# Mixture-of-experts stage of a decoder step: bias rows in four partition groups, the gate read from its bank, gated products moved up, gathers that leave empty slots out

## The reference

```python
logits = (t @ router_w) + router_b
top_v, top_e = lax.top_k(logits, TOP_K)              # 4 of 32 experts for each token
gate = jax.nn.softmax(top_v, axis=-1)
def run_block(tok, g, e):                            # the tokens of one expert
    gu = t_pad[tok] @ w_up[e] + b_up[e]              # (tokens, 2048)
    a = jnp.minimum(gu[:, :D_FF], SWIGLU_LIMIT)      # gate part, limit 7
    u = jnp.clip(gu[:, D_FF:], -SWIGLU_LIMIT, SWIGLU_LIMIT)
    y = ((u + 1.0) * a * jax.nn.sigmoid(1.702 * a)) @ w_down[e] + b_down[e]
    return y * g[:, None]
out = h + sum over the experts of each token of its y
```

## Time and profile before

| | before |
|---|---|
| median of three runs | 1878.54 us |
| the profiled execution's own time | 1879.48 us |
| its span (first to last instruction) | 1877.7 us |
| TensorE matmul (PE) busy | 1830.7 us, 97% |
| TensorE weight load (PEld) busy | 1502.2 us, 80% |
| VectorE (DVE) busy | 1502.5 us, 80% |
| ScalarE (ACT) busy | 1129.8 us, 60% |
| GpSimd (POOL) busy | 245.0 us, 13% |

### The profile page before, as it was taken

The page is one execution under the profiler, slowest core; times in us unless marked ns, Lnnn a source line. Parts: engine busy times, 40 slices in busy tenths (PEclk is TensorE's granted clock), DMA queues, the critical chain, the costliest instruction groups (busy, mean ns, idle before and its releaser), DMA issues.

```text
span 1877.7 us, 27455 instructions
## 1 busy us (share of the span) xinstructions
PE 1830.7 (97%) x9813; PEld 1502.2 (80%) x9813; DVE 1502.5 (80%) x1754; ACT 1129.8 (60%) x1126; POOL 245.0 (13%) x259
## 2 busy tenths in 40 slices
PE   7999999999999999999999999999999999999998
PEld 5898988787768677888888888888888888888886
DVE  6865876644367458999999999999999999999995
ACT  5335544442432346767776776776776777677674
POOL 0040000012330133100110010010011001001000
PEclk9999999999999999999999999999999999999999
DMA  5074221123355249999999999999999999999993
GB/s 227 8 245 168 68 76 51 46 84 96 113 151 196 91 154 370 374 379 383 373 377 388 376 369 390 381 366 385 387 370 373 394 368 371 388 386 369 388 368 106
DMA packets 76747, 514.23 MB, mean 274 GB/s; under 512 B 10744, under 2 KB 31296, under 8 KB 50800
## 3 DMA queue, kind: packets, MB, share of 16 engines
q1 hardware_dynamic: 58944, 454.19, 61.5%
q0 software_dynamic: 17584, 58.51, 11.6%
q10 hardware_dynamic: 144, 0.55, 0.1%
HBM read 490.36 MB, written 28.24 MB: 276 GB/s over the span
## 4 chain that ended last, share of the span: by engine, by line
PE 75%; issue 8%; DVE 7%; ACT 6%; DMA 3%; ACTq 0%; DVEq 0%; POOL 0%; SPq 0%; POOLq 0%
PE bank L1153 26%; PE bank L1171 14%; PE bank L703 6%; PE bank L755 5%; PE bank L630 3%; ACT qT_rounded L1558 3%; PE bank L603 3%; PE bank L1002 3%; PE bank L1135 2%; PE bank L1129 1%; DMA ring<-in_w_exp 1%; PE bank L977 1%; DVE slab L2303 1%; DVE slab L2306 1%; PE bank L1145 1%
## 5 line engine op out<-in xcount | busy, mean ns | idle before, releaser
L2256 DVE TENSOR_TENSOR ring_rounded<-ring,wide_rounded 128x2048 fp32r<-128x2048 f32 x192 | 431.4, 2288 | 50.7 <-ACT wide_rounded L1558 50.3
L1153 PE MATMUL bank<-ring_rounded,slab_rounded 128*128 128x512 f32 x1024 | 400.7, 391 | 0.0
L1558 ACT ACTIVATE wide_rounded<-ring 128x2048 fp32r<-128x2048 f32 x192 | 359.8, 1908 | 10.4 <-PE bank L1153 8.8
L1153 PE MATMUL bank<-xn_rounded,slab_rounded 128*128 128x512 f32 x1024 | 327.5, 391 | 0.0
L2256 DVE TENSOR_TENSOR ring_rounded<-ring,xn_rounded 128x2048 fp32r<-128x2048 f32 x128 | 292.9, 2288 | 16.6 <-ACT xn_rounded L1558 16.6
L1171 PE MATMUL bank<-wide_rounded,slab_rounded 128*128 128x512 f32 x768 | 258.9, 398 | 0.0
L1153 PE MATMUL bank<-wide_rounded,slab_rounded 128*128 128x512 f32 x768 | 247.2, 389 | 0.0
L1558 ACT ACTIVATE xn_rounded<-ring 128x2048 fp32r<-128x2048 f32 x128 | 244.0, 1906 | 0.0
L1153 PEld LDWEIGHTS bank<-ring_rounded,slab_rounded 128*128 128x128 f32 x1024 | 192.6, 188 | 41.5
L1153 PEld LDWEIGHTS bank<-xn_rounded,slab_rounded 128*128 128x128 f32 x1024 | 193.1, 189 | 40.4 <-issue 0.8
L2483 POOL DMA_INDIRECT out_y<-slab,small x32 | 85.1, 2659 | 1001.8 <-ACT slab L1633 1001.8
(11 more groups left out here) (463 smaller groups left out, 2989.3 us busy)
## 6 DMA issues: line engine op xcount, KB each, us to landing
ring<-in_w_exp SPq DMA_DIRECT2D x192, 2048.0 KB, 10.8
ring<-in_w_blk SPq DMA_DIRECT2D x40, 512.0 KB, 3.6
slab<-in_w_tok SPq DMA_DIRECT2D x4, 1304.0 KB, 15.4
ring<-in_w SPq DMA_DIRECT2D x8, 512.0 KB, 3.7
ring<-in_w_out SPq DMA_DIRECT2D x2, 2048.0 KB, 13.4
xn<-in_xT SPq DMA_DIRECT2D x4, 520.0 KB, 8.1
ring<-in_k_cmp SPq DMA_DIRECT2D x32, 64.0 KB, 3.5
ring<-in_k_cmp POOLq DMA_DIRECT2D x32, 64.0 KB, 2.7
```

Source lines behind the costliest of these rows:

```text
L1153: r = mm(bank[:, c, :], a[:, 4 * h + k, :], w[:, k, :], start=False, stop=h == 1 and k == 3 and x == 2)
L1558: fn(WH[(2 * c + h) % 6], ring[:, half_of(c, h)], ACT.Copy).then_inc(S["wh_ready"], 1)
L2256: v.tensor_tensor(ring_r[:, half_of(c, h)], ring[:, half_of(c, h)], WHf[(2 * c + h) % 6], ALU.subtract)\
```

## The change

- PE: the four bias matmuls of an expert are issued together ahead of its first chunk. Each uses 32 partitions only: partition group c (32c to 32c+31) of `pick_r` and `bias_r` holds the rows of bank c, 16 experts with a high and a low row each, and `bias_r` has two column halves (`group`) for the experts 0 to 15 and 16 to 31. PE's loop over the experts is split in two for this. The bank waits (`up_read`) stand at the head of an expert, for all four banks, together with one on `sig_ready`.
- ScalarE: `gated` reads the gate from its PSUM bank, before clipping; the clip is applied to the result by VectorE with GATE_LIMIT. It waits for PE (`half_used`) and not for VectorE, and writes one of two SG buffers. `high_half(5, 0)` moves ahead of `turned_hidden` 0.
- VectorE: both `gate_part` are gone. `hidden_part` 1 moves ahead of `low_half(5, 1)`; `low_half(0, 0)` of the next expert moves behind `low_hidden` 1, and `low_rows` ahead of `low_half(0, 1)`. Three DMA waits move out of the loop.
- Ahead of the experts: the bias comes in one DMA of 128 partitions by 1024 and not in two of 32 by 2048. VectorE builds the new selection matrices from the identity (six small operations), then waits for this DMA and adds a constant row selection to it, all before its first `residual`. ScalarE makes one copy of 128x1024, VectorE one operation of 128x1024; the copies of L1579, L1580, L2277 and L2161 go.
- GpSimd: the gathers get a bound, so that a slot number beyond the last token is left out.

```diff
-            def up_chunk(n, c, last_biases=False):
-                pe.wait_ge(S["up_read"], 4 * n + c + 1)
+            def up_bias(c, group):
+                rows = slice(32 * c, 32 * c + 32)
+                mm(bank[:, c, :], pick_r[rows, :], bias_r[rows, group, :], start=True, stop=False)
+
+            def up_chunk(n, c, group, last_biases=False):
+                first = isinstance(n, int) and n == 0
                 if c == 0:
+                    if not first:
+                        pe.wait_ge(S["sig_ready"], 2 * n)
+                        pe.wait_ge(S["up_read"], 2 * n)
                     pe.wait_ge(S["pick_set"], n + 1)
...
-                q = order[c]
-                mm(bank[:, c, :], pick_r, bias_r[:, q * 512:(q + 1) * 512], start=True, stop=False)
+                if first:
+                    if c >= 2:
+                        pe.wait_ge(*((S["ovf_ready"], 1), (S["y0_ready"], 2 * RT - 2))[c - 2])
+                    up_bias(c, group)
+                elif c == 0:
+                    for b in range(4):
+                        up_bias(b, group)
...
             for t in range(RT):        # ScalarE, first tile's turn
...
                 if t == 0:
-                    act.wait_ge(S["bup_in"], 32)
-                    fn(bias_r[0:NE, :], bias_raw[0:NE, :], ACT.Copy).then_inc(S["bias_ready"], 1)
-                    fn(WH[0][NE:2 * NE, :], bias_raw[NE:2 * NE, :], ACT.Copy).then_inc(S["bias_hi"], 1)
+                    act.wait_ge(S["bias_step"], 1)
+                    fn(WH[0][:, 0:D], bias_raw, ACT.Copy).then_inc(S["bias_step"], 1)
...
             def gated(n, hf):
-                act.wait_ge(S["up_read"], 4 * n + 2 * hf + 5)
-                fn(SG, AA, ACT.Gelu_apprx_sigmoid).then_inc(S["sig_ready"], 1)
+                act.wait_ge(S["half_used"], 12 * n + 4 * hf + 14)
+                fn(SG[hf], bank[:, 2 * hf, :], ACT.Gelu_apprx_sigmoid).then_inc(S["sig_ready"], 1)
...
+                high_half(n, 5, 0)
                 turned_hidden(n, 0)
-                high_half(n, 5, 0)
                 gated(n, 1)
...
+            dve.wait_ge(S["bup_in"], 16)
+            v.tensor_scalar(bias_raw, bias_raw, own_chunk[:, 1:2], None, ALU.add).then_inc(S["bias_step"], 1)
             for t in range(RT):
                 residual(t, 0)
...
             def hidden_part(n, hf):
                 dve.wait_ge(S["half_used"], 12 * n + 4 * hf + 16)
-                v.tensor_scalar(UU[hf], bank[:, 2 * hf + 1, :], LIMIT, -LIMIT, ALU.min, ALU.max).then_inc(S["up_read"], 1)
...
+                v.tensor_scalar(UU[hf], bank[:, 2 * hf + 1, :], 1.0 + LIMIT, 1.0 - LIMIT, ALU.min, ALU.max).then_inc(S["up_read"], 1)
...
-                v.scalar_tensor_tensor(UU[hf], UU[hf], 1.0, SG, ALU.add, ALU.mult).then_inc(S["h_ready"], 1)
+                v.scalar_tensor_tensor(UU[hf], SG[hf], GATE_LIMIT, UU[hf], ALU.min, ALU.mult).then_inc(S["h_ready"], 1)
...
-                gate_part(n, 1)
                 dve.wait_ge(y0_out[0], 32)
                 low_hidden(n, 0)
                 low_half(n, 5, 0)
+                hidden_part(n, 1)
                 low_half(n, 5, 1)
-                hidden_part(n, 1)
                 if following:
                     pick_expert(e + 1)
-                    low_half(n + 1, 0, 0)
...
                 low_hidden(n, 1)
                 if following:
+                    low_half(n + 1, 0, 0)
+                    low_rows(n + 1)
                     low_half(n + 1, 0, 1)
-                    low_rows(n + 1)
...
-            for x in (0, 1):
-                dma(bias_raw[x * NE:(x + 1) * NE, :], d["b_up"]).then_inc(S["bup_in"], 16)
+            dma(bias_raw, d["b_up"]).then_inc(S["bup_in"], 16)
...
                 pool.indirect_dma_start(out=GX[par][:, :], out_offset=None, in_=trow[:, :],
-                                        in_offset=bass.IndirectOffsetOnAxis(ap=index, axis=0))\
+                                        in_offset=bass.IndirectOffsetOnAxis(ap=index, axis=0),
+                                        bounds_check=NT - 1, oob_is_err=False)\
```

More of the change, by code:

```diff
@@ L60 @@
 ALPHA = 1.702
+GATE_LIMIT = LIMIT / (1.0 + math.exp(-ALPHA * LIMIT))
 SLOT = 4096
@@ L306, in build @@
         YR = [slab[:, (6 + b) * D:(7 + b) * D] for b in (0, 1)]
-        AA = slab[:, 8192:8704]
-        SG = slab[:, 8704:9216]
+        SG = [slab[:, 8192 + b * 512:8704 + b * 512] for b in (0, 1)]
         UU = [slab[:, 9216 + b * 512:9728 + b * 512] for b in (0, 1)]
         pick_r = slab_r[:, 10304:10432]
-        pick = causal[:, 0:NE]
+        pick = causal[:, 0:NE].rearrange("p (x j) -> p x j", x=2)
+        low_row = causal[:, 3 * NE:3 * NE + 1]
+        own_chunk = causal[:, 3 * NE + 1:3 * NE + 5]
         entall = causal[:, NE:3 * NE].rearrange("p (e x) -> p e x", x=2)
@@ L377, in halves @@
             return bank[:, 2 * pair:2 * pair + 2, 0:n]
-        order = (0, 2, 1, 3)
         def input_pair(m):
@@ L1173, in down_half, with block_of @@
                 r.then_inc(S["half_used"], 1)
-            def block_of(n, par, following, last_biases=False):
+            def block_of(n, par, following, group, last_biases=False):
                 for c in range(3):
-                    up_chunk(n, c, last_biases and c == 0)
+                    up_chunk(n, c, group, last_biases and c == 0)
                 turn_hidden(n, 0)
-                up_chunk(n, 3)
+                up_chunk(n, 3, group)
                 pe.wait_ge(S["y0_ready"], 2 * RT)
@@ L1192, in block_of @@
                 down_half(n, 5, 1)
[L1194 to L1201, removed]
+            pe.wait_ge(S["bias_ready"], 1)
+            block_of(0, 0, True, 0, True)
+            block_of(1, 1, True, 0)
+            with pe.Fori(1, NE // 4) as pair:
+                block_of(2 * pair, 0, True, 0)
+                block_of(2 * pair + 1, 1, True, 0)
+            with pe.Fori(NE // 4, NE // 2 - 1) as pair:
+                block_of(2 * pair, 0, True, 1)
+                block_of(2 * pair + 1, 1, True, 1)
+            block_of(NE - 2, 0, True, 1)
+            block_of(NE - 1, 1, False, 1)
             pe.wait_ge(S["ovf_ready"], 1)
@@ L1204, in _ @@
             with pe.If(most > P):
[L1205 to L1208, removed]
+                for group in range(2):
+                    with pe.Fori(group * NE // 2, (group + 1) * NE // 2) as e:
+                        for b in range(4):
+                            turn_rows(4 * e + (NE + b), b % 2)
+                            block_of(4 * e + (NE + b), b % 2, False, group)
         @block.scalar
@@ L1641, in _ @@
             act.wait_ge(S["bd_done"], 2 * RT)
+            act.wait_ge(t_out[0], 48)
+            act.wait_ge(y0_out[2], 16)
             block_of(0, 0, True)
@@ L2257, in low_half @@
                     .then_inc(S["wl_ready"], 1)
-            one(v.tensor_tensor(pick, ident[:, 0:NE], ident[:, NE:2 * NE], ALU.add))
+            by_side = ident.rearrange("p (g x j) -> p x j g", g=4, x=2)
+            one(v.tensor_reduce(pick, by_side, AX, ALU.add))
+            one(v.tensor_reduce(low_row, pick[:, 1, :], AX, ALU.add))
+            one(v.tensor_tensor(pick[:, 1, :], pick[:, 1, :], pick[:, 0, :], ALU.subtract))
+            one(v.tensor_copy(pick[:, 0, :], pick[:, 1, :]))
+            one(v.tensor_reduce(own_chunk, ident.rearrange("p (g x) -> p g x", g=4), AX, ALU.add))
+            one(v.tensor_tensor(own_chunk[:, 1:2], own_chunk[:, 1:2], own_chunk[:, 3:4], ALU.add))
             one(v.memset(first_oh[1], 0.0))
+            dve.wait_ge(S["bup_in"], 16)
+            v.tensor_scalar(bias_raw, bias_raw, own_chunk[:, 1:2], None, ALU.add).then_inc(S["bias_step"], 1)
             for t in range(RT):
@@ L2365, in _ @@
             first_rows(RT - 1, 1)
+            dve.wait_ge(t_out[0], 48)
+            dve.wait_ge(t_out[1], 32)
+            dve.wait_ge(y0_out[2], 16)
             with dve.Fori(0, NE // 2 - 1) as pair:
```

30 lines of the change are left out of this document (10 added, 20 removed).

## The result

The changed kernel takes 1854.2 us (median of four runs, 1851.96 to 1858.85). The kernel before, beside it on the same chip, takes 1878.36 (1876.52 to 1879.04). The ratio is 0.9871, with a 95% interval of 0.9859 to 0.9883: 24.2 us faster. The forecast was 1860.9, its range 1852 to 1871. Rival D, which differs from the forecast only in that the row groups overlap wholly, gave 1854.5. That it lies 0.3 from the measured time is partly luck: other terms were off by more than that, and cancelled.

A forecast was written before the change was run, and what follows sets the result against it. The prediction took PE to bound the kernel, with DMA close behind. Its terms, 11.5 + 1.2 + 3.2 + 1.7 = 17.6 us off 1878.54, gave 1860.9 us, range 1852 to 1871.

The forecast's parts named there:

- Rival D: Bias matmuls: the four row groups overlap wholly, gaining 9.6 us and not 3.2, kernel 1854.5 us; chance 0.20.
- The wait (11.5): PE's second turn in each expert: the reorder removes its 0.37 us wait for VectorE's product, 11.5 us gained.
- What is late next is PE itself: Second turn: once VectorE's product comes earlier, nothing but PE holds the path; 0.37 x 31 gained.
- The bias matmuls (3.2): Head of each expert: four 32-partition matmuls cost 0.82 us where four full ones cost 0.92; 3.2 us gained in all.
- The working's 0.94: Bias matmuls: the group's cost in us if each matmul also waited for its own weight load of 0.1.
- The 0.69 of the prediction's side sentence: Bias matmuls: group cost in us by the skill's factor plus the 0.39 drain, a 7 us win.
- The first expert (1.2): First expert's second turn: the reorder and two clips less remove a stall of 1.17 us, 1.2 gained.
- The router (1.7): Ahead of the experts: 2.7 us gained by fewer bias copies, 1.0 lost by waiting for the bias DMA, net 1.7.
- the 1.0 to be lost behind the waiting VectorE: First tile: ScalarE's second sum of squares starts at 624.5, not 623.6, behind VectorE's DMA wait; 1.0 us lost.
- the 2.7 of the copies: First tile's turn: ScalarE's two bias copies, 1.80 + 1.91 us, become one of 1.0; 2.7 gained.
- The gathers (0): GpSimd's gathers: leaving out empty slots relieves DMA by 0 to 1.1 us an expert, worth nothing on PE's path.
- rival B: Experts: DMA takes over as the bound, with a floor of 35.9 us an expert, kernel 1870 us; chance 0.15.

The follow-up runs named there:

- e5: Changed kernel with VectorE's `hidden_part` 1 back behind `low_half(5, 1)`: 1853.84 us, ratio 0.9864.
- e6: Changed kernel with ScalarE's `high_half(5, 0)` back behind `turned_hidden` 0: 1853.09 us, ratio 0.9860.
- e7: Changed kernel with both moves undone, `hidden_part` 1 behind `low_half(5, 1)` and `high_half(5, 0)` behind `turned_hidden` 0: 1867.94 us, ratio 0.9939.
- e10: Kernel before with only ScalarE's `high_half(5, 0)` moved ahead of `turned_hidden` 0: 1868.28 us, ratio 0.9945.
- e9: Kernel before with only VectorE's `hidden_part` 1 moved ahead of `low_half(5, 1)`: 1904.34 us, ratio 1.0136.
- e1: Changed kernel with all four bias matmuls in partition group 0: 1874.22 us, ratio 0.9977.
- e3: Changed kernel with each 32-partition bias matmul at the head of its own chunk: 1915.87 us, ratio 1.0201.
- e12: Changed kernel with the first expert's four bias matmuls issued in two pairs, not one at each chunk: 1850.71 us, ratio 0.985.
- e8: Changed kernel with the next expert's four bias matmuls issued right behind `turn_rows`, not at the head of their own expert: 1854.44 us, ratio 0.9866.
- e4: Changed kernel with the gathers unbounded again, all 128 rows fetched, empty slots too: 1855.74 us, ratio 0.988.

## Why the prediction was right, and where it was not

**The wait (11.5): size exact, account incomplete.** 0.37 an expert went, as said. The working put it to `hidden_part` 1 ahead of `low_half(5, 1)` and called `high_half(5, 0)` only the helper. The runs show two independent ways: in the changed kernel each of them suffices (e5, e6, e7), and on the kernel before `high_half(5, 0)` alone does it (e10), while `hidden_part` 1 alone loses 25 us (e9). The weak step is "What is late next is PE itself". It is so in the changed kernel, but the working looked only at who reads `low_half(5, 1)`; it did not ask what else moves back behind the product. In e9 that is `low_hidden` 1, and PE waits for it. The working neither priced nor named as cover that `low_half(0, 0)` moves behind it.

**The bias matmuls (3.2): mis-sized, 31 x 0.28 = 8.7 measured.** The price of the form was read rightly from the earlier trace rows: 0.39 there, 0.42 here. Taken too high was what the four add: 0.43 was chosen between 0.23 and 0.92, and they add 0.22 to 0.23, the end for whole overlap. (The working's 0.94, for a wait for each weight load, is not the sum of its parts: 0.39 + 0.23 and three or four times 0.1 are 0.92 or 1.02. Nothing hangs on it.) That is rival D, which got a chance of 0.20 for want of a row. It explains most of the distance between 1860.9 and 1854.2: 30 x (0.28 - 0.10) = 5.4. The Trainium skill ("TensorEngine Tiling (Array Packing)", Key Properties) says that a change of tiling mode drains the engine. The price of some 0.42 for each change of form in e1 and e3 agrees with that; that it is a drain no run shows. The factor 3.07 of the Trainium skill ("TensorE: Matmul & The Clock Gate", Measured speedup vs the span model) would give 0.30 for the group, and 0.64 was measured. The 0.69 of the prediction's side sentence, which adds the 0.39, is closer; rival D's 0.62 is closest.

**The first expert (1.2): failed.** The wait of the earlier trace rows did go, but the turn came no earlier. From the first bias matmul to the second turn, before and after, by the busy time of the engines:

```profile
713.58:745.41 31.83, 30.86 (x124) 23.42 (x123) 29.62 (x24) 21.57 (x15) 10.85 (x7) 0.95 0.91 367
```

```profile
706.24:738.35 32.11, 32.11 (x124) 23.42 (x124) 27.35 (x20) 21.50 (x15) 8.32 (x7) 0.95 0.88 335
```

At the same granted clock it is 31.83 with the wait and 32.11 without it. PE's own way there grew from 30.71 (the last matmul's start and 0.23) to 32.11, because here the four bias matmuls stand apart, each with its own change of form, which the working overlooked although it gave the price:

```profile
716.60 0.40 PE L1165 MATMUL bank<-xn_rounded,slab_rounded 128*128 128x512 f32 x1
716.93 0.50 PE L1140 MATMUL bank<-oT_rounded,slab_rounded 32*128 32x512 f32 x1
717.36 0.50 PE L1165 MATMUL bank<-wide_rounded,slab_rounded 128*128 128x512 f32 x1
717.70 0.39 PE L1165 MATMUL bank<-ring_rounded,slab_rounded 128*128 128x512 f32 x1
```

That is 1.10 instead of three times 0.23, so 0.41 more, and nearly the same for the third chunk. The first bias matmul, behind small transposes, costs some 0.2 more than before, the fourth, behind a turn, 0.4: 1.4 in all, against the 1.17 gained. Nor was it the reordering that took the wait away: in e7, with both moves undone, PE does not wait at this turn either, since it wants the product 32.14 behind the first bias matmul and VectorE has it at 31.86. e12 shows the price in this place.

**The router (1.7): 2.6 from the change, some 1.4 with the clock.** VectorE and ScalarE in order of time, the first tile:

```profile
617.39 0.75 DVE L2284 TENSOR_SCALAR oT<-oT,small 128x1024 f32<-128x1024 f32 x1 [2.81 <-DMA oT<-in_b_up]
618.06 0.67 DVE L2190 SCALAR_TENSOR_TENSOR slab<-bank,wide 8x512 f32<-8x512 f32 x1
...
619.47 0.68 DVE L2190 SCALAR_TENSOR_TENSOR slab<-bank,wide 8x512 f32<-8x512 f32 x1 [0.74 <-PE bank L1002]
```

```profile
622.42 1.04 ACT L1595 ACTIVATE xn_rounded<-oT 128x1024 fp32r<-128x1024 f32 x1
```

All stands 3.4 us earlier than in the trace of before. The DMA lands near its forecast place (621.3 - 3.4 = 617.9), the addition takes 0.75 and not 1.2, and the second residual is where it was (619.47 + 3.4 = 622.87). So the 1.0 to be lost behind the waiting VectorE wasn't; the one copy takes 1.04 as said. From `out_part` to the first bias matmul the stretch is 102.3 before and 98.3 after. The granted clock differs too, 0.95 of full speed over it before and 0.97 after. The traces of e5 and e8, with 0.95, take 99.8: at an equal clock 2.6 is the change's, close to the 2.7 of the copies. The rest, 1.4, goes with the clock; why the changed kernels mostly see less low clock is not shown.

**The gathers (0): right**, and rival B wrong at its root. It took the DMA engines' busy time, 35.56 an expert, for a need. In e4, with all rows gathered, the bytes of an expert fit into 99.8% of 35.30 = 35.23.

## What to carry to other kernels

Going into a form of fewer rows and out again has a fixed price each time (0.42 us here); put small matmuls of different row groups side by side in one change of form, and never one by one between full ones. When a product is late, look first at what makes the operation ahead of it late: one earlier rounding on another engine did what the reordering was meant to do. A stall that is removed gives its whole length only if the engine that stalled gets there no later than before. Price each reordering on its own against who reads the operations it pushes back, since a move that is free inside a set of moves can cost 25 us alone.

## What the runs showed of the hardware that was not expected

- Four matmuls of 32 rows in four row groups cost what one alone costs (0.64 and 0.655), for rounded fp32r data with 512 columns. In one row group each further one costs 0.22 to 0.23, half of the 0.43 that unrounded data shows.
- The DMA engines were 99.8% busy over a thousand us (e4), and neither PE nor ScalarE waited for a load: their busy share alone doesn't say that they are the bound.
- The start of the first `out_part` varied by 4 us and the low-clock time of the router stage from trace to trace, in kernels that are the same up to there. A term of 2 us ahead of the experts can't be read from one pair of traces.
